# Two layers of a diffusion backbone on one core: the norms between sub-layers as two streams of tokens, three PSUM slots everywhere

## The reference

```
_pre(x)  = rmsnorm(x, g) * (1 + scale) + shift                 # scale, shift: one number per channel,
_post(x) = x + weight * gate * rmsnorm(y, g)                   # one set for context, one for latent tokens
layer:   x = _post(x, swiglu(_pre(x)))          # 1024 -> 2 x 2816 -> 1024
         x = _post(x, mixer(_pre(x)))           # half state-space heads, half Fourier heads, then w_out
         x = _post(x, swiglu(_pre(x)))
```

## Time and profile before

| | |
|---|---|
| median of three runs | 2869.12 us (2868.15 to 2871.70) |
| the profiled execution: its time | 2866.32 us |
| the profiled execution: its span, first to last instruction | 2864.4 us |
| PE busy | 2680.7 us, 94% of the span |
| DVE / ACT / POOL busy | 1677.3 / 716.3 / 821.0 us |
| mean granted clock of TensorE | 0.969 of full speed |

### The profile page before, as it was taken

How to read it: one execution, slowest core, us unless ns; L and a number is a source line. 1 busy time by engine, 2 the same in 40 slices (tenths; PEclk the granted TensorE clock), 3 DMA queues, 4 the chain that set the end, 5 groups by cost and what they waited for, 6 DMA issues and landing times.

```text
span 2864.4 us, 39514 instructions
## 1 busy us (share of the span) xinstructions
PE 2680.7 (94%) x16446; PEld 2496.0 (87%) x16446; DVE 1677.3 (59%) x2235; ACT 716.3 (25%) x977; POOL 821.0 (29%) x1292
## 2 busy tenths in 40 slices
PE   5899999998899889999999799999998898899996
PEld 4899999997869789999999699999998766588885
DVE  5868877865582686766665743343434683644444
ACT  4211121113413421111111322112122413322222
POOL 1258775732050200000000228767551050100001
PEclk9999999999999999999999899999999999899998
DMA  9443444442455134343441232222233455133321
GB/s 314 125 132 125 152 152 128 129 165 87 151 147 162 45 111 125 111 130 114 132 126 52 74 74 87 95 94 89 94 103 120 138 167 161 57 96 99 96 89 59
DMA packets 340459, 337.09 MB, mean 118 GB/s; under 512 B 52529, under 2 KB 311225, under 8 KB 336697
## 3 DMA queue, kind: packets, MB, share of 16 engines
q1 hardware_dynamic: 279224, 204.07, 24.3%
q10 hardware_dynamic: 51840, 77.07, 8.0%
q0 software_dynamic: 9216, 53.42, 5.0%
HBM read 290.02 MB, written 44.50 MB: 117 GB/s over the span
## 4 chain that ended last, share of the span: by engine, by line
PE 81%; DVE 11%; ACT 3%; DMA 2%; issue 2%; SPq 1%; POOL 0%; DVEq 0%; ACTq 0%; POOLq 0%
PE ps L454 71%; DVE adaW L541 3%; PE ps L1390 2%; PE ps L582 2%; PE ps L1089 2%; ACT wH L439 1%; PE ps L1415 1%; DVE tmpN L1168 1%; DMA y_d<-YC 1%; DVE wL L446 1%; DVE rmsX L1177 1%; DVE xT L1049 1%; PE ps L1404 1%; DMA xin<-in_x_dram 1%; PE ps L1074 1%
## 5 line engine op out<-in xcount | busy, mean ns | idle before, releaser
L454 PE MATMUL ps<-hH,wH 128*128 128x384 f32 (+1 forms) x2928 | 1019.9, 348 | 67.9 <-DVE hL L1186 48.1
L454 PE MATMUL ps<-hL,wH 128*128 128x384 f32 (+1 forms) x2928 | 1011.6, 345 | 0.0
L454 PE MATMUL ps<-hH,wL 128*128 128x384 f32 (+1 forms) x2928 | 1010.9, 345 | 0.0
L446 DVE TENSOR_TENSOR wL<-raw,wH 128x1024 fp32r<-128x1024 f32 x300 | 392.0, 1319 | 551.9 <-ACT wH L439 551.3
L454 PEld LDWEIGHTS ps<-hH,wH 128*128 128x128 f32 x2928 | 556.1, 190 | 95.6 <-issue 55.9
L454 PEld LDWEIGHTS ps<-hL,wH 128*128 128x128 f32 x2928 | 556.3, 190 | 18.1
L454 PEld LDWEIGHTS ps<-hH,wL 128*128 128x128 f32 x2928 | 555.5, 190 | 18.5
L454 PE MATMUL ps<-midH,wH 128*128 128x384 f32 (+1 forms) x1232 | 426.2, 346 | 12.7 <-DVE wL L446 9.9
L454 PE MATMUL ps<-midH,wL 128*128 128x384 f32 (+1 forms) x1232 | 423.6, 344 | 0.0
L454 PE MATMUL ps<-midL,wH 128*128 128x384 f32 (+1 forms) x1232 | 423.2, 344 | 0.0
L439 ACT ACTIVATE wH<-raw 128x1024 fp32r<-128x1024 f32 x300 | 310.8, 1050 | 448.2 <-PE ps L454 399.3
(11 more groups left out here) (257 smaller groups left out, 2382.3 us busy)
## 6 DMA issues: line engine op xcount, KB each, us to landing
raw<-in_ffn_gu_dram SPq DMA_DIRECT2D x176, 512.0 KB, 3.8
adaW<-in_w_ada_dram ACTq DMA_DIRECT2D x40, 1536.0 KB, 7.0
raw<-in_ffn_down_dram SPq DMA_DIRECT2D x88, 512.0 KB, 3.7
x_d<-xT POOLq DMA_DIRECT2D x4, 3072.0 KB, 9.6
xT<-x_d POOLq DMA_DIRECT2D x4, 3072.0 KB, 11.1
W_d<-gW POOLq DMA_DIRECT2D x16, 512.0 KB, 4.0
VT_d<-gVT ACTq DMA_DIRECT2D x16, 512.0 KB, 3.0
raw<-in_w_in_dram SPq DMA_DIRECT2D x16, 512.0 KB, 6.2
```

Of the source, the lines that this page charges most:

```text
L446: nc.vector.tensor_tensor(wL[:, n % SPLIT_SLOTS, :], raw[:, n % RAW_SLOTS, :], wH[:, n % SPLIT_SLOTS, :].bitcast(f32), ALU.subtract).then_ ...
L454: ins = nc.tensor.matmul(dst, a, b, start=first and n == 0, stop=last and n == 3 * len(pairs) - 1)
```

## The change

1. **Seams in two halves of the tokens.** `part(tok0, h)` gives half h: columns 0 to 383 and 384 to 767 (in M1's last products and F21 256 each). The last down pair and the last six w_out tiles are multiplied half by half, the first half of all tiles first. All of the seam is done per half, with TensorE's small sums and spreads in banks 6 and 7. On VectorE the residual of the second half is cut: its chunks 0 to 3 stand ahead of the next input of the first half, its chunks 4 to 7 between that input's chunks. `first_groups` multiplies the first half of all 8 chunks, then the second.
2. **x is normed as y was**: GpSimd adds the squares, and the wide products and the wide reciprocal are gone. All additions to x are VectorE's.
3. **Three slots everywhere**: `F.slots = 3`, and three in the mixer's output part.
4. **Rides** stand at the up tiles (i = 1, 3), a tile later than before. ScalarE takes the columns and issues the next load between VectorE's reading of the up tile and `midH`; before it did so ahead of the gate tile's Silu. The first ride's steps stand behind `up(1)` and `up(3)` on VectorE, before they stood ahead of them.
5. In F10 and F11 the small products for the mixer (`head_weights`) stand ahead of the last down pair, and ScalarE's copy of them ahead of the seam.

```diff
-        F.slots = 3 if gen else 4
+        F.slots = 3
...
-        pe.wait_ge(w_lo, base + count)
-        for k in range(KC):
-            pe.wait_ge(h_lo, KC * pre.nth + k + 1)
-            for u in range(count):
-                wh, wl = wtile(base + u)
-                for i, (t0, w) in enumerate(halves(pre.tok0)):
+        for u in range(count):
+            pe.wait_ge(w_lo, base + u + 1)
+        for h in range(2):
+            t0, w = part(pre.tok0, h)
+            for k in range(KC):
+                if pre.after and h == 1 and k == 0:
+                    x_stat(pe, pre, 1)
+                    x_spread(pe, pre, 1)
+                pe.wait_ge(h_lo, 2 * KC * pre.nth + h * KC + k + 1)
+                for u in range(count):
...
-                ride = F.ride0 + 2 * s + i // 2 if F.ride0 is not None and i % 2 == 0 else None
+                ride = F.ride0 + 2 * s + i // 2 if F.ride0 is not None and i % 2 else None
...
-        def up(i, f):
+        def up(i, g, f, ride):
 
             act.wait_ge(up_read, F.n0["up_read"] + f + 1)
+            if ride is not None:
+                take_columns(act, ride, 2 * tile_slot(F, g), TOK // 2)
+                next_ride(ride + 2)
             nc.scalar.activation(midH[:, f % 4, F.tok0:TOK], midF[:, f % 2, F.tok0:TOK], ACT.Copy).then_inc(mid_hi, 1)
...
         for j in range(2):
+            split_lo(dve, F.base + 2 * j + 3)
+            up(2 * j + 1, 2 * j + 1, j)
             if F.ride0 is not None:
                 ada_steps(dve, F.ride0, j * KC, (j + 1) * KC)
-            split_lo(dve, F.base + 2 * j + 3)
-            up(2 * j + 1, 2 * j + 1, j)
...
+    def last_down(pe, F):
+
+        n = F.base + 6 * NPH - 2
+        pe.wait_ge(w_lo, n + 2)
+        pe.wait_ge(mid_lo, F.n0["mid_lo"] + FC)
+        (ah, al), (bh, bl) = wtile(n), wtile(n + 1)
+        s0 = (FC - 2) % 4
+        for h in range(2):
+            for m in range(KC):
+                if m >= F.slots:
+                    pe.wait_ge(last_read, F.n0["last_read"] + KC * h + m - F.slots + 1)
...
+                if h == 1 and m == 2:
+                    y_stat(pe, F.post, F, 0)
+                if h == 1 and m == 4:
+                    y_spread(pe, F.post, 0)
...
+    def norms_vector(dve, N, S, nxt):
...
+        for i in range(2 * KC):
+            h, m = divmod(i, KC)
+            if m == 0:
+                dve.wait_ge(bc_x, nth_of(N, h) + 1)
+            scale_h(dve, nxt, h, m, source)
+            if i and i != KC:
+                rest_h(dve, nxt, (i - 1) // KC, (i - 1) % KC)
+            if h == 0 and m % 2:
+                new_x(dve, N, 1, 4 + m // 2)
+            if i == KC - 1:
+                last_squares(dve, N, 1, sq_x, sumX, sum_x, all_x)
+                rest_h(dve, nxt, 0, KC - 1)
+                invert(dve, N, 1, sd_x, rs_x)
+        rest_h(dve, nxt, 1, KC - 1)
```

563 lines of the change are left out of this document (360 added, 203 removed).

## The result

| | before | changed |
|---|---|---|
| median | 2868.64 us (4 runs, 2864.69 to 2871.70) | 2895.19 us (4 runs, 2890.83 to 2899.51) |
| ratio to before | | 1.0093, 95% interval 1.0076 to 1.011 |
| the profiled execution: time, span | 2866.32, 2864.4 us | 2899.51, 2897.7 us |

The changed kernel is slower by 26.6 us in the medians (by 33.2 in the two profiled executions, of which the changed one is the longest of its four). I had said 2882, with a range of 2858 to 2898 and .68 for slower.

The account below looks back on a forecast made before the run. VectorE and its chain of sums were taken to decide at seams, TensorE elsewhere. Gains of 14.6 and losses of 29.8 made it 15.2 us slower, 2881.5 with time around the span; it said 2882, range 2858 to 2898.

Parts of the forecast that it names:

- Three slots and `midH`: Down pairs: the fourth tile waits for VectorE's first reading, with midH .43 later; losses 6.7 (F20), 3.9 (F10), 9.2 us (F21).
- Rival B: The slots don't wait in the down pairs, so 19.8 us of loss fall away: 2862, chance .16.
- Rides: Later columns gain 3.9 us; the first ride's later steps lose .7 in F10 and 1.7 in F20.
- +3.9: Waits for adaW: rides wanted 8.3 us later win 3.9 of the 4.9 us outside the single 6.6 us wait.
- The fourth weight: Behind the seams, clearing yT delays the weight's low part: loss of 1.8 us each in F20 and F11, 1.5 in F21.
- The seams: Halves start earlier, but VectorE paces: gains 4.5 (to F11), 2.0 (F20), .9 (M1), losses .7 (M0), .5 us (F21).
- .29: Seam F20 to F11: the residual's share in VectorE's time for each first-half chunk, .29 us of about 2.0.
- Rival A: Seams: the early start carries through if VectorE's first-half chunk pace is under 1.56 us; 2841, half of it 2861; chance .14.
- What the cut costs VectorE: Seams: halved scales and additions cost VectorE 6.9 us a seam by trace rows, 5.1 by the skill's fixed latency.
- Rival C: Seams: more low clock, as thin first-half work at 1.2 GHz adds 7 to 14 us: 2888 to 2896, chance .20.
- The end: After the last seam: last x earlier and two blocks left instead of four, 36.5 us against 39.8, a gain of 3.3.
- my own forecast: Whole kernel, without the rivals: 2874 to 2888 us, chance .50.

Follow-up runs that it names:

- experiment 9: Changed kernel with TensorE's sum of the second half's squares of x moved ahead of the first half's last chunk: 2885.36 us, ratio 1.0069 to the kernel before.
- experiment 8: Changed kernel with the second half's residual chunks 4 to 7 behind all hL of the first half, not between them: 2887.67 us, ratio 1.0073 to the kernel before.
- the extra products: Changed kernel with small unread 128-column products in TensorE's waits of the five seams: 2886.94 us; the same added to a kernel with all repairs: 2840.21 us.
- three edits that each won nothing: Changed kernel with rides as before (2893.38 us), first groups' end weight by weight and clearing split (2891.42), or ride load earlier (2894.73); with all repairs 2843.91.

## Why the prediction was right, and where its sum was short

**Three slots and `midH`: right, and the largest loss.** I had 6.7 in F20 and 9.2 in F21; it is 8.0 and 10.8. The changed kernel's timeline at a pair of F20 (ACT takes the columns and issues the load, then `midH`; VectorE's first reading; PE's fourth tile) and of F21:

```profile
1099.98 0.17 ACT L621 ACTIVATE modraw<-ps 128x6 f32<-128x6 f32 x1 [8.89 <-DVE midF L804]
...
1100.41 0.85 ACT L768 ACTIVATE midH<-midF 128x768 fp32r<-128x768 f32 x1 [0.25 <-issue]
...
1104.78 0.95 DVE L821 TENSOR_TENSOR yT<-ps,yT 128x768 f32<-128x768 f32 x1
...
1105.78 0.45 PE L480 MATMUL ps<-midH,wH 128*128 128x384 f32 x1 [0.59 <-DVE yT L821]
1106.06 0.34 PE L480 MATMUL ps<-midL,wH 128*128 128x384 f32 x1
...
2549.04 0.50 PE L480 MATMUL ps<-midH,wH 128*128 128x512 f32 x1 [0.78 <-DVE yT L821]
```

The pair begins at 1098.79: the reading is 5.99 behind it (5.56 before, and .43 for the two moved instructions), the fourth tile 6.99, where 6.24 was due. That is the .74 a pair that I had; what it missed is that the fourth tile's products then start again slowly, the second .28 us behind the first, where .17 is the pace, .14 in all. In F10 the term was wrong: I had put 3.9 us on a later `midH` at its nine pairs, and the waits for a down tile's reading fell there from 2.9 us in nine to 2.1 in four, since at the other five pairs a weight came later still (next paragraph). Rival B is out: the slots wait.

**Rides: the step that failed is "+3.9".** The stall at tile 5 of F10 is 7.6 us (I had 7.7), F20's 2.31 in place of .53, so 1.8 (I had 1.7). But the other columns' gain did not stay: the waits for `adaW` in F10's further rounds, 3.9 us, are gone, and 9.2 us of waits for `wL` stand ahead of five of its pairs, the longest 4.5. The term counted later columns as slack and left out that their taking issues the next load, so the load moved with them. VectorE (steps, then the weight's low part) and PE at the longest of these waits:

```profile
262.15 0.42 DVE L568 TENSOR_SCALAR adaP<-adaW,siluC 128x384 f32<-128x384 f32 x1 [6.58 <-DMA adaW<-in_w_ada_dram]
...
266.65 1.42 DVE L472 TENSOR_TENSOR wL<-raw,wH 128x1024 fp32r<-128x1024 f32 x1
...
268.12 0.69 PE L480 MATMUL ps<-midH,wH 128*128 128x384 f32 x1 [4.50 <-DVE wL L472]
```

The load was issued at 251.23, and VectorE stood idle until it had landed; the low part of the pair's weight stands behind the ride's eight steps. This happens in all nine further rounds of F10, 43.8 us of idle VectorE, where the kernel before has none. It is read from the timeline; no run moves these loads alone. F10 is 6.0 us longer in the profile, where I had .7, and of the 6.0 some 3 is within what that stage differs by itself.

**The fourth weight: right in sign, wrong in the main cause.** I had put 1.8 on the clearing of `yT`. VectorE and ScalarE at the end of the seam to F11:

```profile
1672.35 6.35 DVE L795 MEMSET yT<- 128x768 f32 x8
1679.59 1.23 DVE L472 TENSOR_TENSOR wL<-raw,wH 128x1024 fp32r<-128x1024 f32 x1 [0.89 <-ACT wH L465]
...
1677.80 0.81 ACT L758 ACTIVATE sgate<-ps 128x768 f32<-128x768 f32 x1 [4.91 <-PE ps L480]
1678.51 1.05 ACT L465 ACTIVATE wH<-raw 128x1024 fp32r<-128x1024 f32 x1
```

The clearing ends at 1678.70, and VectorE waits .89 us more for the high part, which ScalarE makes behind a Silu that unit 0's last product releases. Before, unit 0 was used up 2.1 us ahead of the end, with the chunk's two halves side by side; now 1.0. This makes 1.03 in F11 (2.15 for 1.12) and 1.12 in F20. Without the clearing the weight would come no earlier, for its high part is there only at 1679.56; with an earlier high part it would come .89 earlier, at the clearing's end. The rest of F11's 2.6 is a slower clock behind the wait (below).

**The seams: the term that was short by 12 us.** I had gains of 4.5, 2.0 and .9 (to F11, F20 and M1) and losses of .7 and .5 (to M0 and F21), together +6.2; it is +2.9, -2.4, -1.6, -3.2 and -1.4 (67.39 against 66.04), together -5.7. The early start was there: the first products of the five first groups (to M0, F20, F11, M1 and F21) come 12.5, 11.8, 13.6, 14.5 and 5.5 us earlier than before, 58 in all, where I had 47. More than all of it is lost again behind them. In the seam to F11, counted from the pair's start, the first product is at 41.8 (I had 42.6), the first half's last chunk begins at 59.1 (57.8), the second half's first product is at 65.0 (63.8) and the end at 79.4 (77.8):

```profile
1658.53 0.44 PE L480 MATMUL ps<-hH,wH 128*128 128x384 f32 x1 [1.97 <-DVE hL L1323]
...
1660.21 0.72 PE L1131 MATMUL ps<-ones,sumX 128*128 128x1 f32 x6
...
1664.44 0.45 PE L480 MATMUL ps<-hH,wH 128*128 128x384 f32 x1 [2.01 <-DVE hL L1323]
```

The first half takes 17.3 us from its first chunk to its last, and I had 15.2. My ".29" for the residual between the chunks is half of an addition (.58) alone; half of its scale, .30, was left out, and over seven chunks that is the missing 2.1 us. The seams to M0, F20 and M1 have the same 17.3. The second half then takes 14.4 us, where I had 12.5 and beside them 1.5 for products at the low clock; in the seam to F20 it takes 15.6. The sum behind the last chunk was in my queues at that place, so it is no part of the miss, but it is a loss that nothing demands, as experiment 9 shows. That its seams come out at 72.3, 76.4 and 72.3, where I had forecast 72.4, 77.8 and 72.4 for the order without it, is a coincidence. Rival A's mechanism, the first half's chunk pace, was tested by experiment 8 and does not decide.

What the cut costs VectorE: a scale is now .74 + .61 us for 1.14, an addition 2 x .55 for .96, which over 24 and 8 of them is 6.2 us, where my rows gave 6.9. The estimate worked out from the Trainium skill, "VectorE: DVE Perf Modes", section "The TRN2 errata", was 5.1; the measured cost lies between the two. By either price the forecast is below the measured time, not above it.

**Rival C was real, as an addition.** The clock in the seams fell from .84 to .86 down to .75 at the mixers' and stayed at .83 at F11's, and the extra products won 8 us of the 27 (intervals just overlapping). By the Trainium skill, "TensorE: Matmul & The Clock Gate", section "What's actually happening", the throttled state is the default and activity releases it; thin first halves agree with that, as far as one can see in a mean clock.

**The end: right**, 4.2 us won for 3.3.

In sum: slower, and for the largest loss by the mechanism that I had named; the gain at the seams and of the later rides did not come, and so 26.6 us where I had 13. In the profiles it is 33.2 for 15.2, and of the 18 between them the seams make 12, F10 5, F20's first part 2.5 and the pairs of F20 and F21 3; the rest goes the other way. That 2895 lies inside the range is in part luck: it is outside the 2874 to 2888 that I gave my own forecast, in the part that was there for rival C, and what the extra products won is 8 us. Two sums were wrong as well: 2881.5 and 2.8 are 2884.3, not 2883, and the first product's lead in the seam to F11 stands as 12 and as 11.3, where 55.5 less 42.6 is 12.9.

## What to carry to other kernels

When work is cut in two streams, each stream brings its own chain of sum, root, reciprocal and spread, and every short step of it must stand in its queue ahead of the bulk work that it releases the next half for; here one small sum moved ahead of 9 products was worth some 7 us, about a quarter of the loss. A slot fewer is priced by one subtraction, the end of the reader's first reading against (slots) x (tile time): that gave the fourth tile's start within .03 us in F20 and F21, and .14 a pair for the restart came on top. When a step moves, ask what it triggers: the columns taken later also issued the next load later, and VectorE stood still for it. A wait that is taken away is worth nothing until the next late thing is named: three edits that each won nothing won 7.3 us in one place when made together (4.3 with the extra products beside them).
